# Filler products on constants in four waits of TensorE, and head sums and head spreading as full 128x128 products

## What is computed

```python
# second block, time mixer: r, k, v and low-rank projections, then
kk = (k * k_k).reshape(bsz, seq, H, N)
kk = kk / max(norm(kk, axis=-1), 1e-12)          # per head: a sum over 64 features
... # decay, rate, gate from low-rank products; scan over the tokens
y = (y - mean) * rsqrt(var + GN_EPS) * gn_g + gn_b   # per head again
out = ((y + bonus) * g) @ w_o
# third block: nsa_compress turns 16 windows of keys (and of values) into 15 compressed ones
```

## Time and profile before

| | us |
|---|---|
| median of 3 runs | 3061.32 (3055.65 to 3062.4) |
| profiled execution: its own time | 3062.81 |
| profiled execution: its span | 3061.0 |
| PE busy in it | 2906.7 (95%), PEld 2700.3 |
| DVE, ACT, POOL busy | 1704.8, 1430.4, 165.4 |
| share of PE in the chain that ended last | 80% |
| mean granted clock of TensorE | 0.975 |

### The profile page before, as it was taken

How to read it: one execution, slowest core, us unless ns; L and a number is a source line. 1 busy time by engine, 2 the same in 40 slices (tenths; PEclk the granted TensorE clock), 3 DMA queues, 4 the chain that set the end, 5 groups by cost and what they waited for, 6 DMA issues and landing times.

```text
span 3061.0 us, 53742 instructions
## 1 busy us (share of the span) xinstructions
PE 2906.7 (95%) x23664; PEld 2700.3 (88%) x23664; DVE 1704.8 (56%) x1977; ACT 1430.4 (47%) x1817; POOL 165.4 (5%) x197
## 2 busy tenths in 40 slices
PE   8999898999998998999999999999987999999998
PEld 8988898999998898999989899899877889876887
DVE  5564555545554556455455654554767454575555
ACT  4455655444455655444445344444551244454444
POOL 1000100000000010001000000000002000054000
PEclk9999999999999999999999999999979999997999
DMA  6553334554553344556554445455420145551453
GB/s 248 189 181 134 138 133 159 192 187 173 192 179 125 137 152 152 191 181 223 191 204 168 153 178 191 171 189 184 151 107 3 48 177 187 179 181 43 152 185 132
DMA packets 69393, 492.87 MB, mean 161 GB/s; under 512 B 7853, under 2 KB 9421, under 8 KB 10534
## 3 DMA queue, kind: packets, MB, share of 16 engines
q1 hardware_dynamic: 64224, 465.53, 42.5%
q10 hardware_dynamic: 4938, 23.92, 2.1%
HBM read 488.32 MB, written 1.06 MB: 160 GB/s over the span
## 4 chain that ended last, share of the span: by engine, by line
PE 80%; DVE 8%; ACT 7%; POOL 2%; issue 2%; PEld 0%; DMA 0%; ACTq 0%; PEldq 0%; DVEq 0%; POOLq 0%; SPq 0%
PE front L105 52%; PE acc L105 28%; ACT weights_hi L118 3%; DVE weights_lo L313 2%; POOL conv_gate L3193 1%; POOL conv_out L3196 1%; DVE tmp L690 1%; DVE h L683 1%; DVE h L698 1%; PEld acc L105 0%; ACT L1111 0%; ACT tmp L1111 0%; DVE b_x_lo L522 0%; ACT b_att_w_by_query L1013 0%; DVE b_x_lo L750 0%
## 5 line engine op out<-in xcount | busy, mean ns | idle before, releaser
L313 DVE TENSOR_TENSOR weights_lo<-weight_ring,weights_hi 128x2048 fp32r<-128x2048 f32 x440 | 1010.0, 2296 | 916.8 <-ACT weights_hi L118 916.5
L105 PE MATMUL front<-b_x_hi,weights_hi 128*128 128x256 f32 x3568 | 1011.0, 283 | 15.5 <-DVE b_x_lo L750 9.9
L118 ACT ACTIVATE weights_hi<-weight_ring 128x2048 fp32r<-128x2048 f32 x440 | 839.7, 1909 | 388.7 <-PE acc L105 355.1
L105 PE MATMUL front<-b_x_hi,weights_lo 128*128 128x256 f32 x3568 | 1005.4, 282 | 0.0
L105 PE MATMUL front<-b_x_lo,weights_hi 128*128 128x256 f32 x3568 | 1004.9, 282 | 0.0
L105 PEld LDWEIGHTS front<-b_x_hi,weights_hi 128*128 128x128 f32 x3568 | 675.3, 189 | 28.9 <-issue 13.3
L105 PEld LDWEIGHTS front<-b_x_lo,weights_hi 128*128 128x128 f32 x3568 | 675.8, 189 | 3.3
L105 PEld LDWEIGHTS front<-b_x_hi,weights_lo 128*128 128x128 f32 x3568 | 674.9, 189 | 0.0
L105 PE MATMUL acc<-weights_hi,b_hidden_hi 128*128 128x512 f32 x832 | 329.6, 396 | 0.0
L105 PE MATMUL acc<-weights_hi,b_hidden_lo 128*128 128x512 f32 x832 | 328.2, 394 | 0.0
L105 PE MATMUL acc<-weights_lo,b_hidden_hi 128*128 128x512 f32 x832 | 327.3, 393 | 0.0
(11 more groups left out here) (493 smaller groups left out, 3904.1 us busy)
## 6 DMA issues: line engine op xcount, KB each, us to landing
weight_ring<-in_weights SPq DMA_DIRECT2D x440, 1024.0 KB, 4.8
xn<-in_norm_rows ACTq DMA_DIRECT2D x14, 1024.0 KB, 4.8
sgu_bias_row<-in_sgu_rows ACTq DMA_DIRECT2D x1, 2048.0 KB, 10.9
sgu_norm_rows<-in_sgu_rows ACTq DMA_DIRECT2D x1, 2048.0 KB, 9.9
bias_hankel<-bias_scratch ACTq DMA_DIRECT2D x1, 1536.0 KB, 6.5
h<-in_x SPq DMA_DIRECT2D x2, 512.0 KB, 6.6
mem_norm<-in_memory SPq DMA_DIRECT2D x1, 1024.0 KB, 14.1
sgu_w_spatial<-in_sgu_w_spatial ACTq DMA_DIRECT2D x1, 1024.0 KB, 4.7
```

What stands on the lines that cost most here:

```text
L105: return pe.matmul(out, a, b, start=start, stop=stop, skip_group_check=True)
L118: return act.activation(out, in_, ACT.Copy, scale=scale)
L313: dve.tensor_tensor(k.w.lo[:, n % 2, :], k.ring[:, n % RING, :], k.w.hi[:, n % 2, :], ALU.subtract) \
```

## The change

`pe_warm` is called at four more places: 14 products before the three projections (bank 3), 24 before `pe_pairs(0)` and 12 before `pe_pairs(1)` (bank 3), and 14 before `pe_compress_turn(0)` (bank 5). Beside that `head_of` becomes a 128x142 constant of which 128x128 slices are taken, so that `pe_sum_heads` fills 128 output rows (112 of them zero); `head_rows`, `head_numbers` and `gn_row` take 128 partitions (the rows of `head_rows` from 16 on are zero), so that `pe_to_features` contracts over 128 rows. ACT's square root, DVE's maximum and reciprocal and POOL's multiplication run over 128 partitions in place of 16, with the same elements for each, and the three transfers bring 512 KB in place of 64.

```diff
-        "head_of": colm % 16 == 2 * (colm // 16) + row // 64,
+        "head_of": np.arange(14 + P)[None, :] == 14 + row // 64,
...
-    k.head_numbers = k.rstd[0:16, :]
+    k.head_numbers = k.rstd[:, :]
...
-        k.head_rows["kk"] = k.sb(own, "head_rows_kk", [16, D])
+        k.head_rows["kk"] = k.sb(own, "head_rows_kk", [P, D])
...
-        k.head_rows["y"] = k.sb(own, "head_rows_y", [16, D])
-        k.gn_row = k.sb(own, "rwkv_gn_g_row", [16, D])
+        k.head_rows["y"] = k.sb(own, "head_rows_y", [P, D])
+        k.gn_row = k.sb(own, "rwkv_gn_g_row", [P, D])
...
 def pe_sum_heads(k, pe, of, x, ready, taken, bank):
-    out = empty(k, pe, bank, taken)[0:16, 0:S]
+    out = empty(k, pe, bank, taken)[:, 0:S]
...
-        i = mm(pe, out, k.con("head_of")[:, 16 * q:16 * q + 16], x[:, q, :], q == 0, q == KT - 1)
+        i = mm(pe, out, k.con("head_of")[:, 14 - 2 * q:14 - 2 * q + P], x[:, q, :], q == 0, q == KT - 1)
...
         pe_to_features(k, pe, "kk", 4, lambda p: ("kk", 2 * p + 1))
 
+    pe_warm(k, pe, 14)
     for j in range(3):
...
-            act.activation(k.head_numbers, k.bank[4][0:16, 0:S], ACT.Sqrt).then_inc(*k.s.up("head_std", "kk"))
+            act.activation(k.head_numbers, k.bank[4][:, 0:S], ACT.Sqrt).then_inc(*k.s.up("head_std", "kk"))
...
 def pe_pairs(k, pe, pp):
+    if pp < 2:
+        pe_warm(k, pe, (24, 12)[pp])
     pe.wait_ge(*k.s.at("front", pp, "k"))
...
-    act.dma_start(k.gn_row[:, :], bass.AP(tensor=k.aps["rwkv_gn_g_row"].tensor, offset=0, ap=[[0, 16], [1, D]])) \
+    act.dma_start(k.gn_row[:, :], bass.AP(tensor=k.aps["rwkv_gn_g_row"].tensor, offset=0, ap=[[0, P], [1, D]])) \
...
-    act.activation(k.head_numbers, k.bank[0][0:16, 0:S], ACT.Sqrt, bias=k.eps(64e-5)[0:16], scale=1 / 64) \
+    act.activation(k.head_numbers, k.bank[0][:, 0:S], ACT.Sqrt, bias=k.eps(64e-5), scale=1 / 64) \
...
 def pe_compress_turn(k, pe, e):
+    if e == 0:
+        pe_warm(k, pe, 14, 5)
     pe.wait_ge(*k.s.at("cmp_rows", e))
...
-        "head_rows": np.repeat(np.eye(16, dtype=np.float32), 64, axis=1),
+        "head_rows": np.repeat(np.eye(P, 16, dtype=np.float32), 64, axis=1),
```

## The result

| | before | after |
|---|---|---|
| median, us | 3060.88 (3055.65 to 3062.4, 4 runs) | 3037.61 (3036.36 to 3042.7, 4 runs) |
| profiled execution: time, span | 3062.81, 3061.0 | 3042.7, 3040.9 |
| ratio after / before | | 0.9928, 95% interval 0.9913 to 0.9944 |

The account below looks back on a forecast made before the run. PE was taken to bound the kernel (80% of the span), losing time at half clock and in waits. Terms summed to +0.8 us on 3062.81, 3063.6, less 1.5 for the median: 3062.1, range 3056.5 to 3067.5.

Parts of the forecast that it names:

- Head sums with 128 columns: Head sums of kk and y: 0.1 us lost for kk, longer constant table included, and 0 for y.
- the rest of 0.05: Remaining chance, 0.05: the clock is also kept at places beyond the edited ones, giving a time below 3055 us.
- Projections and kk: 14 products before the projections gain 0.3 us; spreading kk over 128 rows holds the clock and gains 3.1.
- Rival D: Rows of zeros do not hold the clock, or 1.76 us of idle drags it down: 3065.2 us, chance 0.12.
- Pairs: 24 and 12 products before the pairs: start late behind bank 3, 3.3 us late, 1.1 given back, 2.2 lost.
- Rival B: Late products on constants do not matter, since DVE and ACT have slack behind both places: 3058.0 us, chance 0.23.
- Rival C: Products on constants stay at half clock throughout, at first pairs and compress turn: slower, 3068.2 us, chance 0.13.
- Compress turn: 14 products before the compress turn wait for bank 5: 2.8 us late, 0.9 absorbed by POOL's wait, 1.9 lost.
- The sum of the edits: All edited places together: -3.1 + 0.1 + 0 - 0.3 + 2.2 + 1.9 = +0.8 us.

Follow-up runs that it names:

- e1_pad14: Before plus 14 unused zero columns behind the constants, moving every buffer allocated behind them by 64 bytes: 3044.72 us, ratio 0.9945.
- e8: Before with 64 bytes free ahead of the pair b2_x and 192 behind it, so b2_x moves 64 and what follows in block 2 moves 256: 3036.27 us.
- e9: Before with 192 bytes free ahead of the split weights and 64 behind, so weights move 192 and everything behind them 256: 3037.68 us, ratio 0.9923.
- e7_pad48: Before plus 48 unused constant columns, moving the buffers behind them by 192 bytes: 3056.2 us, ratio 0.9989.
- e3_four_warms: Before plus only the four runs of products on constants, head sums and spreading as before, old addresses: 3058.83 us, ratio 0.9992.
- e11: e10_placed with all edits of the change, head_of sharing zero columns so that nothing moves: 3014.92 us, ratio 0.9848.
- e12: e10_placed with the full-row and full-column head sums and spreading, without the four runs of products on constants: 3010.07 us, ratio 0.983.
- e2: The changed kernel with all edits, but head_of sharing 14 zero columns of down_32, so every buffer keeps its old address: 3056.14 us, ratio 0.9988.
- e4: Before plus 64 unused constant columns, moving the buffers behind them by 256 bytes: 3057.19 us, ratio 0.999.
- e6: Before plus 32 unused constant columns, moving the buffers behind them by 128 bytes: 3055.98 us, ratio 0.9995.
- e5_pad8: Before plus 8 unused constant columns, moving the buffers behind them by 32 bytes: 3037.56 us, ratio 0.9929.
- e10_placed: Before, program unedited, with unused columns placing 256-column operands and hidden pairs at the lowest-pitch addresses in all blocks: 3013.14 us, ratio 0.9842.

## Why the prediction was wrong

**The step that failed** is half a sentence of "Head sums with 128 columns": "The longer constant table at the start of the program is inside this 0.1." I priced the longer table as a longer transfer, and never asked what lies behind it. By e1_pad14 what lies behind it is worth 13 of the 20 us between the two profiled executions, and 16 of 23 in the medians. No rival named it. The measured time does lie in the rest of 0.05, below 3055, but that was about the clock. Beside it a second error, of the range: the three runs shown spread over 6.75 us, 29 runs of before over 22 (3047.97 to 3070.43), and a single profile was used as if each of its half-clock stretches were the kernel's.

**What the pitch is not.** Not the clock, which is 1.00 over the rows shown of before, after, e8 and e9. Not the other engines' writes into the weights either: in block 2 of before, from 1775 to 1960, the 256-column pitch is 118.6 ns while neither ACT nor DVE splits a unit, 118.7 while DVE does and 118.6 while ACT does, from 258, 399 and 336 pairs of products. What suggests itself is TensorE's own two reads, the moving operand and the next weight load beside it; that they get into each other's way is inferred from e8 and e9 and not seen in a row. The Trainium skill (TensorE: Matmul & The Clock Gate, section "Step-by-step: what each phase is for") says that the two have ports of their own, so that loading the next tile's weights takes no read bandwidth from the running product. The runs here are hard to square with that, though they don't show which read waits for which: by the distance between the two operands alone the pitch goes from 113.5 to 120 ns at the same clock, up to 6%. Why d decides, and why a group at d = 192 takes one rhythm or the other, stays open. So does most of the loss in block 1, which after, e1 (both +8.7) and e9 (+10.1), all at d = 224 there, and e7_pad48 (+8.8, at d = 96) have and kernels at the old addresses don't (-0.1 to +4.3). A part of it grows evenly over the dense products, in after from +4.5 us at 611 us to +5.7 at 891, which fits the slower pitch; the rest comes in steps, of which e3_four_warms, at the old addresses, has some too.

**Point by point, the steps on the edits.** Columns are those of the same views of before.

*Projections and kk*, timeline of after, to hold against the earlier trace rows, then the window around the spreading, to hold against the second of the earlier trace rows:

```profile
2159.00 3.29 PE L105 MATMUL front<-cons 128*128 128x128 f32 x28
2163.07 0.36 PE L105 MATMUL front<-rwkv_x_hi,weights_hi 128*128 128x256 f32 x1 [0.78 <-DVE rwkv_x_lo L522]
...
2238.90 3.69 PE L105 MATMUL acc<-rstd,head_rows_kk 128*128 128x256 f32 x16 [1.82 <-issue]
...
2248.35 0.42 DVE L2143 COPY act_gate<-front 64x256 f32<-64x256 f32 x1 [1.50 <-PE front L105]
```

```profile
2237.00:2245.00 8.00, 6.18 (x39) 5.66 (x39) 7.96 (x16) 4.26 (x6) 0.00 (x0) 1.00 0.37 132
```

Right. The 14 products (28 records) begin where PE falls idle, take 3.29 us, and the first real product waits 0.78 where it waited 3.51; the clock stays up; and nothing comes of it, -0.5 in after, in e3 -0.4, and -0.5 in e1, which lacks the edit. The spreading runs at clock 1.00 in 3.69 us, and DVE's copy follows its start by 2248.35 - 2238.90 = 9.45 us, in before by 12.57: 3.1 earlier, as forecast. In the table the stretch is -3.5 and -3.3 with the edit, +0.5 to -0.2 without; in the kernels outside it, -3.5 and -5.0 with it (e11, e12) and -1.8 to +1.4 without. Rival D is out, and full 128-column loads cost nothing that shows.

*Pairs*, after and then e3_four_warms, to hold against the earlier trace rows:

```profile
2284.63 8.09 PE L105 MATMUL front<-cons 128*128 128x128 f32 x48 [4.43 <-ACT rwkv_e_neg_cum L2218]
...
2293.82 1.29 DVE L2293 TENSOR_TENSOR rwkv_pairs_b<-acc,cons 128x512 f32<-128x512 f32 x2 [3.63 <-PE acc L105]
...
2295.49 2.94 PE L105 MATMUL front<-cons 128*128 128x128 f32 x24
```

```profile
2290.02 8.36 PE L105 MATMUL front<-cons 128*128 128x128 f32 x48 [4.43 <-ACT rwkv_e_neg_cum L2218]
...
2299.48 1.29 DVE L2293 TENSOR_TENSOR rwkv_pairs_b<-acc,cons 128x512 f32<-128x512 f32 x2 [3.90 <-PE acc L105]
```

Right in its mechanism, and the sizes hold: the 24 products start only behind ACT's exponential (2290.02, forecast 2290.03), take 8.09 and 8.36 us (forecast 7.8), and DVE, which had no pause there, waits 3.63 and 3.90 (forecast 3.3); the 12 hide. From the unit split at 2288.11 to that at 2434.35 the edit costs +4.0 us in e3, +1.8 in e2, -1.0 in e11 and -3.0 in after; kernels without it scatter from -0.9 to +2.4 (e9). Forecast: +2.2, between -0.9 and +5.9. What is given back differs: behind the pairs after has no half-clock stretch up to 2450, where before has three. Rival B, that the late products don't matter, is out for DVE's wait and stays possible for the time. Rival C, half clock throughout, had 10.3 us for the 24; with 8.09 and 8.36 it is out here (at the compress turn, its other place, it is not: see below).

*Compress turn*, after, to hold against the earlier trace rows:

```profile
2730.82 0.50 ACT L118 ACTIVATE b_att_w_by_key<-acc 128x384 f32<-128x384 f32 x1
...
2731.37 6.05 PE L105 MATMUL acc<-cons 128*128 128x128 f32 x28 [4.18 <-ACT b_att_w_by_key L118]
2737.35 1.06 PE L105 MATMUL acc<-cons,cmp_rows 16*128 16x16 f32 x8
...
2773.43 1.03 PE L105 MATMUL acc<-conv_out,cons 128*128 128x256 f32 x4
```

Right in its mechanism, but the products are 1.1 us longer than forecast. The products want bank 5 and start at 2731.37, as ACT's copy ends at 2730.82 + 0.50; they take 6.05 us, 14 x 0.43, at half clock for all but the last half microsecond, as rival C had it, where I had 4.9; PE no longer waits for POOL at conv_sum (no idle time at 2773.43). The stretch is 3.2 to 3.9 us longer than in before, and 0 to 1.5 in kernels without the edit: some 2.5 where I had 1.9.

*What I read as the kernel's and was the run's.* Of the nine kernels after and e1 to e8, five (e2 and e3 with edits ahead, e4, e6 and e7 without) are 3.8 to 4.5 us earlier at the split at 2288.11 than at that of 2257.09, by less work at half clock in the stretch at 2278.34; the others are level with before within 0.4. And a stretch at 2786.9 of 17.1 us, which the forecast did not use, is in no other profile: all others of this study have 0 to 10 us at half clock there. First before: the window of that stretch, and conv_gate's products, the first behind it. Then e4_pad64, which has no edit: a window at each of the two places, then conv_sum's products, which stand ahead of the second place (in before the last of them are at 2784.33), and conv_gate's:

```profile
2784.00:2806.00 22.00, 21.67 (x72) 12.95 (x72) 9.52 (x32) 6.54 (x24) 2.66 (x4) 0.61 0.00 1
...
2806.99 1.13 PE L105 MATMUL acc<-conv_gate,cons 128*128 128x256 f32 x4 [0.72 <-ACT cmp_w_by_key L118]
```

```profile
2277.50:2298.00 20.50, 13.07 (x170) 11.04 (x174) 12.48 (x25) 9.30 (x17) 1.99 (x2) 0.67 0.15 53
2784.00:2806.00 22.00, 19.11 (x342) 12.56 (x342) 13.36 (x42) 13.19 (x36) 4.18 (x6) 1.00 0.01 2
...
2783.79 1.03 PE L105 MATMUL acc<-conv_out,cons 128*128 128x256 f32 x4
...
2799.44 1.13 PE L105 MATMUL acc<-conv_gate,cons 128*128 128x256 f32 x4 [0.72 <-ACT cmp_w_by_key L118]
```

The clock reads 0.61 over 22 us in before and 1.00 in e4_pad64; in the first row of e4, 0.67 against the 0.50 of before. From the end of conv_sum's products to the start of conv_gate's, before takes 2806.99 - 2785.03 = 22.0 us and e4 2799.44 - 2784.82 = 14.6, with no edit between them. This is the larger part of why after, e2, e3 and e4 all seem to gain 8 to 10 us between 2768.91 and 2877.00. A comparison of two single profiles would have put that gain down to the products on constants ahead of it.

**The sum of the edits** was +0.8 us. Measured: -4.2 between the medians (0 to -7.6) at the old addresses, +1.8 at the better ones. The first interval leaves +0.8 just out, so the edits did a little better there than forecast, and which term gave that is not settled. But this is a few microseconds; most of the 23 us is the shift behind the constant table, which the sum did not have.

## What to carry to other kernels

When an edit changes the size of any tensor, list what is allocated behind it and whether its address changes modulo 256, and hold that fixed when the edit's own worth is to be measured (pad to a multiple of 256 bytes, as e4_pad64 did); otherwise a shift of 64 bytes can pass for the edit. In a kernel bound by TensorE, try the address of the moving and stationary operands as a tuning knob of its own: here it gave 45 us, 1.5%, for a dozen lines that compute nothing. And lay two traces against each other at one repeated instruction before reading any single place: a gain that grows evenly over stages without an edit is not the edit's.

## What the runs showed of the hardware

- The pitch of fp32r products depends on how their two operands lie to each other in a partition, modulo 256 bytes: 113.5 to 120 ns for 256 moving columns and 228 to 234 ns for 512, at full clock, best with the moving rows at d = 192 and the stationary hidden pair at d = 0 (table above).
- The pitch comes in levels (113.5, 116.7, 117.3, 117.8, 118.3, 118.6, 120.0 ns), and a group of 96 products keeps one: the means of a group's four quarters lie within 1.2 ns of each other in 54 of 56 groups of after. At d = 192 two levels occur in the same execution, 113.5 and 117.8. e5_pad8, with block 1 there, spreads over 19 us in 7 runs; e10_placed, where 28 of 34 groups of block 2 run at 113.5, over 2.3 us in 4. That the levels make the spread is not shown: before, with nothing at d = 192, spreads over 22 us in 29 runs.
